# A shorter ring for gathered expert rows: seven places instead of nine

## The chip, the cores and the metric

The kernel runs on one core of one Trainium2 chip. The metric is the device time of one execution in microseconds (us), lower is better. TensorE (PE) has a matmul side and a weight-load side (PEld). VectorE is DVE, ScalarE is ACT, GpSimd is POOL, and SyncE is SP. SP issues most of the plain transfers, ACT some of them, and POOL all gathers and scatters by index. All of them run on the core's 16 DMA engines.

## The reference

One inference step of a one-layer encoder on 1024 prompt frames and 32 frames of a running stream, in float32. Per frame: one input projection; two attentions, a stick-breaking one and a latent one (MLA); a gated merge and a layer norm give `h`. Then comes the feed-forward part, in which each frame picks experts out of 16384:

```python
s = einsum('thcd,hckd->thck', q, peer_sub_keys)      # 8 heads, 2 x 128 sub-keys
s1, i1 = top_k(s[:, :, 0], 16); s2, i2 = top_k(s[:, :, 1], 16)
top_s, top_pos = top_k(s1[..., :, None] + s2[..., None, :], 16)
act = gelu(einsum('thkd,td->thk', peer_u[experts], xb))
out = einsum('thk,thkd->td', softmax(top_s) * act, peer_v[experts])
y = layer_norm(ALPHA * h + out)
```

So each frame reads 8 x 16 = 128 rows of `peer_u` and 128 of `peer_v`, of 1024 numbers each.

## The kernel before

**Two ways through the experts.** For the frames of three tiles (tiles 1, 2 and 3, 128 frames each) all 16384 experts are computed as matrix products, in 128 iterations of 128 experts. This is the last stage, `dense_experts`. In an iteration `it`, PE multiplies a block of key columns with the frames (L1809, 16 matmuls), ACT takes the gelu (L1843), DVE multiplies with gates (L1876), and 20 iterations later PE multiplies with the value rows (L1798, 12 matmuls). SP loads the key columns (512 KB), gates (192 KB) and value rows (512 KB) of every iteration. For the other five prompt tiles and the 32 frames of the stream the chosen rows are gathered: 672 gathers, each of one row of 2048 numbers (`peer_u` and `peer_v` joined, 8 KB) for each of 128 partitions, which is 1 MB.

**The ring.** A gathered row lies in a ring of `RING = 9` places. Its steps are numbered. In step s DVE first makes the dot product of row s with `h` (L574), then, `LAG = 4` steps late, adds row s-4, weighted, to the sum (L586). Between the two, ACT takes the gelu and the weight (L531, L537). L586 counts the semaphore `used`; POOL waits for it and gathers the next row into the place that came free (L431):

```python
for p, (kind, x) in enumerate(self.places):          # lay_out
    step = x + self.LAG if kind == "row" else ...
    freed.setdefault(step, []).append(p + self.RING)
...
for p in self.fetch_at.get(s, []):                   # pool
    pool.wait_ge(self.used, p - self.RING + 1)
    self.fetch(pool, p)
...
dve.wait_ge(self.got[p % self.RING], self.landed[p]) # dve_row, ahead of L574
```

**What sets the order.** The background work (the steps of the ring, and the routes) is spread over the stages of frame groups 1 and 2 and over the dense stage by the table `SHARES` and by `lay_out`. A route is the choice of 16 experts for one head of one tile: 12 small pieces of DVE work (`route_stage`, L646 to L676). It must be done when step `row` is laid out if `routed_before(row)` asks for it: `u = min(row + self.RING - self.LAG + 5, ...) // TOPK`. Where the share alone has not brought them by then, all 12 pieces stand in one block, once in 16 rows. In the dense stage part(it) hands out DVE's background work in proportion to PE's iterations. POOL runs through the same list: scores, gathers, and 384 scatters of gates (L454), in one order.

**Stick-breaking attention** (`stick_attend`) works on items of 128 x 512. PE computes scores into one of six PSUM banks (L936), ACT takes exp and ln (L1016 to L1024), DVE makes the softplus into one of `S = 6` buffers (L1048) and a running sum into one of `R = 8` (L1065), and PE adds both to the scores two pairs later (L952, L954). DVE waits with `s_done >= t - S + 1` before it writes a softplus buffer again. PE's order in turn u is: `later(2u-4)`, `later(2u-3)`, values, and then `scores(u)`, which fills items 2u and 2u+1.

Of the kernel before, what the change touches and what calls it, by code (L numbers as in the profile page):

```python
# [89 lines left out]
def hybrid_stream_step(nc, a):  # L90
# [21 lines left out]
    with ExitStack() as s:  # L112
        m["zero_done"], = sems(nc, s, "dense_gates_zeroed")
        m["x_in"], m["w0_in"], m["sig0_in"], m["sub0_in"] = sems(
            nc, s, "next_xT_in", "next_w_in_in", "next_gates_in", "next_sub_keys_in")
        m["wq_in"] = sems(nc, s, "next_wq_in_a", "next_wq_in_b")
        m["wo0_in"] = sems(nc, s, "next_w_o_in_a", "next_w_o_in_b")
        m["hTd_in"], = sems(nc, s, "dense_hT_in")
        m["out_stored"], m["mla_stored"], m["hT_stored"] = sems(nc, s, "keys_and_values_stored", "mla_stored", "dense_hT_stored")
        m["gate_stored"] = sems(nc, s, *[f"gate_stored{i}" for i in range(4)])  # L120
        m["h_stored"] = sems(nc, s, "h_stored_a", "h_stored_b")
        m["scores_stored"] = sems(nc, s, *[f"scores_stored{i}" for i in range(SCORE_STAGES)])
        m["keys_in"] = sems(nc, s, *[f"key_columns_in{i}" for i in range(5)])
        bg = Experts(nc, mem, s, a, m)
        spaces = [foreground(mem, g) for g in groups]
        for g in groups:
            f = spaces[g.n]
            project(nc, mem, a, m, f, g, bg, groups[:g.n])
            stick_attend(nc, mem, a, m, f, g, bg, groups[:g.n + 1])
            mla_project(nc, mem, a, m, f, g, bg)  # L130
            mla_attend(nc, mem, a, m, f, g, bg)
            merge_norm(nc, mem, a, m, f, g, bg)
            score_experts(nc, mem, a, m, f, g, bg, list(zip(groups, spaces))[g.n + 1:g.n + 2])
        dense_experts(nc, mem, a, m, bg)
# [34 lines left out]
class Experts:  # L169
# [1 line left out]

    RING, LAG = 9, 4
    NORM_AFTER = 10
    IDS = 176
    SLOTS, FLATS = 22, 8
# [724 lines left out]
def stick_attend(nc, mem, a, m, f, g, bg, upto):  # L902
    bg.begin(g.n, "stick")
    with ExitStack() as s:
# [6 lines left out]
                for par in range(2):  # L911
                    items.append((i, nq, key, rows, vt, diag, par, x == len(tiles) - 1))
        N = len(items)
        E, S, R, A = 4, 6, 8, 4
        work = lambda name, first, n: [mem.at(f"{name}{n * g.n + i}", FG + 38912 + 2048 * (first + i), [P, 512]) for i in range(n)]
        e = work("abs_exp_ln", 0, E)
        sp_ = work("softplus", E, S)
# [1039 lines left out]
```

## Time and profile before

| | |
|---|---|
| Median of 3 runs | 3517.1 us (3508.93 to 3527.14) |
| Span of the profiled execution | 3512.8 us, from its first to its last instruction |
| Median less that span | 4.3 us |
| PE / DVE / POOL / ACT busy | 85% / 69% / 45% / 35% |
| DMA | 1098.51 MB, mean 313 GB/s |
| Gathers (queue q0 with the scatters) | 751.05 MB |

Busy time is the union of an engine's instructions. A share of DMA of 1.00 means that all 16 engines were moving packets all the time. A releaser is the work whose end let an idle engine go on. Windows are in microseconds from the start of the span. The first matmul of the last scores stage starts at 1849, the first of the dense stage at 1959.

### The profile page before, as it was taken

How to read it: one execution, taken by the hardware profiler on the slowest of the kernel's cores; microseconds unless marked ns; L12 is line 12 of the kernel's file. 1: busy time of each engine (PE TensorE's matmuls, PEld its weight loads, DVE VectorE, ACT ScalarE, POOL GpSimd, SP SyncE). 2: the span in 40 equal slices, each digit the busy share in tenths (PEclk: the TensorE clock that was granted, in tenths of full speed). 3: DMA queues.
4: the chain of work that ended last, by engine and by line, in shares of the span. 5: the costliest groups of instructions: out<-in, count | busy, mean ns of one | idle time of the engine just before them, and what ended most of it. 6: DMA issues, size and time to landing. Idle time of an engine off the chain costs nothing. (4 is left out here: it accounts for less than half of the span.)

```text
span 3512.8 us, 36200 instructions
## 1 busy us (share of the span) xinstructions
PE 2979.5 (85%) x10191; PEld 1650.8 (47%) x10191; DVE 2437.9 (69%) x5110; ACT 1219.7 (35%) x3224; POOL 1569.2 (45%) x1186
## 2 busy tenths in 40 slices
PE   8989999775789896776799858999989999989994
PEld 5754745442445454434445534444444444444431
DVE  0122069887686878877696638878778778788878
ACT  0241234665533436765642212222222222222211
POOL 0000035667663288868766763333333333333321
PEclk9988999896899998887899979999999999999997
DMA  4675589667799997676699979999999999999996
GB/s 146 215 256 178 174 330 405 209 196 210 234 342 360 322 379 219 173 203 199 200 360 377 322 239 390 410 399 399 401 399 406 398 398 408 383 410 405 412 381 261
DMA packets 375912, 1098.51 MB, mean 313 GB/s; under 512 B 91712, under 2 KB 210208, under 8 KB 289568
## 3 DMA queue, kind: packets, MB, share of 16 engines
q0 software_dynamic: 165072, 751.05, 57.5%
q1 hardware_dynamic: 176800, 303.85, 24.6%
q10 hardware_dynamic: 33840, 41.30, 3.3%
q8 instruction: 82, 1.34, 0.1%
q14 instruction: 118, 0.97, 0.1%
HBM read 1031.97 MB, written 63.02 MB: 312 GB/s over the span
## 5 line engine op out<-in xcount | busy, mean ns | idle before, releaser
L431 POOL DMA_INDIRECT expert_rows<-in_experts,picked_index x640 | 780.9, 1220 | 1256.1 <-DVE ff_sum L586 1126.5
L586 DVE SCALAR_TENSOR_TENSOR ff_sum<-expert_rows,coefficients,ff_sum 128x1024 f32<-128x1024 f32 x672 | 860.2, 1280 | 163.1 <-ACT coefficients L537 162.0
L574 DVE SCALAR_TENSOR_TENSOR expert_rows<-expert_rows,h_tile 128x1024 f32<-128x1024 f32 x672 | 818.8, 1218 | 196.1 <-DMA expert_rows<-in_experts,picked_index 176.3
L1809 PE MATMUL dense_act_ps<-dense_hT,key_columns 128*128 128x384 f32 x2048 | 709.4, 502 | 140.7 <-DMA key_columns<-in_key_columns 116.8
L454 POOL DMA_INDIRECT gates_by_expert<-dense_gate,gate_address x384 | 681.4, 1774 | 146.6 <-issue 114.2
L1798 PE MATMUL dense_out_ps<-dense_value_rows,dense_weights 128*128 128x512 f32 x1536 | 681.1, 595 | 10.0 <-DVE dense_weights L1876 7.8
L1809 PEld LDWEIGHTS dense_act_ps<-dense_hT,key_columns 128*128 128x128 f32 x2048 | 392.7, 195 | 474.3 <-DMA key_columns<-in_key_columns 183.6
L1798 PEld LDWEIGHTS dense_out_ps<-dense_value_rows,dense_weights 128*128 128x128 f32 x1536 | 292.9, 191 | 357.6 <-issue 318.8
L842 PE MATMUL proj_ps<-xT,w_in_block 128*128 128x384 f32 (+1 forms) x1392 | 419.1, 464 | 28.8 <-PEq L1612 15.6
L842 PEld LDWEIGHTS proj_ps<-xT,w_in_block 128*128 128x128 f32 x1392 | 266.1, 192 | 180.8 <-issue 33.9
L1843 ACT ACTIVATE dense_weights<-dense_act_ps 128x384 f32<-128x384 f32 x128 | 62.5, 489 | 773.4 <-PE dense_act_ps L1809 769.4
L531 ACT ACTIVATE activated<-dots 128x1 f32<-128x1 f32 (+1 forms) x631 | 124.4, 197 | 518.8 <-DVE expert_rows L574 479.1
L1668 PE MATMUL peer_q_ps<-hT,wq_half 128*128 128x384 f32 (+1 forms) x768 | 240.9, 474 | 15.1 <-DMA wq_half<-in_peer_wq 6.9
L1668 PEld LDWEIGHTS peer_q_ps<-hT,wq_half 128*128 128x128 f32 x768 | 149.3, 197 | 97.8 <-issue 16.6
L537 ACT ACTIVATE coefficients<-activated,expert_gate 128x1 f32<-128x1 f32 x640 | 184.1, 294 | 20.2 <-ACT activated L531 0.9
L378 ACT ACT_TABLE_LOAD x110 | 141.1, 1283 | 143.0 <-DVE top_scores L663 54.3
L407 POOL DMA_DIRECT2D expert_scores<-peer_scores x72 | 67.4, 936 | 206.5 <-POOLq L1612 206.4
L1296 PE MATMUL score_ps<-mla_kT,mla_qT 96*128 96x512 f32 (+4 forms) x208 | 107.1, 638 | 39.4 <-PEq L1071 39.4
L1313 PE MATMUL mla_ps_turned<-identity,probs 128*128 128x128 f32 (+2 forms) x312 | 65.1, 326 | 83.7 <-ACT probsT L1352 78.4
L1525 PE MATMUL out_ps<-w_out,mergedT 128*128 128x512 f32 (+1 forms) x288 | 127.6, 593 | 0.0
L1048 DVE SCALAR_TENSOR_TENSOR softplus<-log_weight_ps,abs_exp_ln 128x512 f32<-128x512 f32 (+2 forms) x78 | 50.8, 651 | 104.0 <-ACT abs_exp_ln L1024 101.1
L531 ACT ACT_TABLE_LOAD x90 | 115.5, 1283 | 18.6 <-DVE expert_rows L574 15.8
(192 smaller groups left out, 2957.6 us busy)
## 6 DMA issues: line engine op xcount, KB each, us to landing
key_columns<-in_key_columns SPq DMA_DIRECT2D x128, 512.0 KB
dense_value_rows<-in_experts SPq DMA_DIRECT2D x128, 512.0 KB
gates_by_expert<-zeros POOLq DMA_DIRECT2D x12, 2048.0 KB, 21.9
wq_half<-in_peer_wq SPq DMA_DIRECT2D x48, 512.0 KB
dense_gates<-gates_by_expert SPq DMA_DIRECT2D x128, 192.0 KB
w_in_block<-in_w_in ACTq DMA_DIRECT2D x18, 1024.0 KB
w_in_block<-in_w_in SPq DMA_DIRECT2D x18, 1024.0 KB
w_out<-in_w_out SPq DMA_DIRECT2D x24, 512.0 KB, 7.2
```

Source lines behind the costliest of these rows:

```text
L378: act.preload_act_table_set(EXP_LN)
L431: pool.indirect_dma_start(to, None, self.a["experts"], bass.IndirectOffsetOnAxis(ap=index[:, k:k + 1], axis=0)).then_inc(self.got[p % self ...
L454: pool.indirect_dma_start(self.a["gates_by_expert"], bass.IndirectOffsetOnAxis(ap=self.flat[i][:, k:k + 1], axis=0), self.dgate[i][:, k:k ...
L531: act.activation(self.gel[:, k:k + m], self.dots[:, k:k + m], ACT.Gelu).then_inc(self.gelud, m)
L537: act.activation(self.coef[:, c:c + 1], self.gel[:, c:c + 1], ACT.Identity, scale=gate[:, c:c + 1]).then_inc(self.weighed, 1)
L574: dve.scalar_tensor_tensor(place, place, 1.0, self.h[n % 2][:], ALU.mult, ALU.mult, accum_out=self.dots[:, s % TOPK:s % TOPK + 1]).then_in ...
L586: dve.scalar_tensor_tensor(total, self.ring[:, p % self.RING, D:2 * D], self.coef[:, y % TOPK:y % TOPK + 1], total, ALU.mult, ALU.add).the ...
L842: mm = nc.tensor.matmul(out[:, 0:W], w[b % 2][:, k, col:col + P], xT[:, k, :], start=(k == 0), stop=(k == KC - 1))
L1525: mm = nc.tensor.matmul(ps[2 * n + c][0:r, :], f["mergedT"][:, k, at:at + r], w_out[:, k, 512 * c:512 * (c + 1)], start=(k == 0), stop=(k ...
L1668: mm = nc.tensor.matmul(qp[2 * (h % 2) + c][:, 0:W], wq[h % 4][k // 4][:, k % 4, PKEYS * c:PKEYS * (c + 1)], f["hT"][:, k, :], start=(k == ...
L1798: mm = nc.tensor.matmul(out[d][:, 512 * half:512 * (half + 1)], w[e % AB][:, P * d:P * (d + 1)], vals[e % VB][:, 512 * half:512 * (half + ...
L1809: mm = nc.tensor.matmul(up[it % 2][:, 0:W], keys[it % KB][:, k, :], hTd[:, k, :], start=(k == 0), stop=(k == KC - 1))
```

## The change

The ring of gathered rows has seven places instead of nine; `LAG` stays 4. In stick-breaking attention the softplus has four buffers instead of six, and the running sum six instead of eight. Places in memory move with them, the instructions stay the same. `routed_before` contains `RING`, so a route is demanded two rows later than before.

```diff
-    RING, LAG = 9, 4
+    RING, LAG = 7, 4
...
-        E, S, R, A = 4, 6, 8, 4
+        E, S, R, A = 4, 4, 6, 4
```

## Rows read from the trace of the kernel before

**Rows 1.** The page, busy tenths in 40 slices of the span:

```profile
PE   8989999775789896776799858999989999989994
...
DMA  4675589667799997676699979999999999999996
```

**Rows 2.** Windows: engines, granted clock, DMA share and rate by stretch:

```profile
core 0: us, PE busy (x) PEld busy (x) DVE busy (x) ACT busy (x) POOL busy (x), PEclk, DMA share, GB/s
...
1849.00:1959.00 110.00, 96.75 (x353) 61.08 (x354) 69.98 (x88) 28.53 (x98) 78.38 (x52) 0.93 1.05 383
1959.00:2165.00 206.00, 156.51 (x433) 86.31 (x434) 114.72 (x223) 44.09 (x126) 120.17 (x87) 0.88 0.86 301
2165.00:3256.00 1091.00, 1018.88 (x2689) 510.57 (x2688) 880.45 (x1599) 255.76 (x873) 388.00 (x325) 0.99 1.00 401
3256.00:3480.00 224.00, 191.85 (x464) 88.51 (x464) 184.40 (x317) 44.43 (x158) 69.08 (x60) 0.95 0.97 384
```

**Rows 3.** Groups by line in 2165:3256 (xcount, busy us, mean ns, idle before):

```profile
L1809 PE MATMUL dense_act_ps<-dense_hT,key_columns 128*128 128x384 f32 x1537 | 530.7, 499 | 78.9 <-DMA key_columns<-in_key_columns 78.8
L1798 PE MATMUL dense_out_ps<-dense_value_rows,dense_weights 128*128 128x512 f32 x1152 | 510.0, 592 | 0.0
L586 DVE SCALAR_TENSOR_TENSOR ff_sum<-expert_rows,coefficients,ff_sum 128x1024 f32<-128x1024 f32 x299 | 382.6, 1279 | 85.7 <-ACT coefficients L537 85.1 <-DVEq L620 0.5
L431 POOL DMA_INDIRECT expert_rows<-in_experts,picked_index x300 | 373.4, 1245 | 701.8 <-DVE ff_sum L586 671.7 <-issue 27.7 <-DVEq L620 2.4
L574 DVE SCALAR_TENSOR_TENSOR expert_rows<-expert_rows,h_tile 128x1024 f32<-128x1024 f32 x300 | 366.1, 1220 | 89.4 <-DMA expert_rows<-in_experts,picked_index 88.1 <-ACT activated L531 0.5
```

**Rows 4.** All instructions on expert_rows, first and last start:

```profile
L574 DVE SCALAR_TENSOR_TENSOR expert_rows<-expert_rows,h_tile x672: 1203/1217/1283, 470.3 to 3470.7; 128x1024 f32<-128x1024 f32 x168
...
L431 POOL DMA_INDIRECT expert_rows<-in_experts,picked_index x640: 937/1175/2038, 461.9 to 3460.9; - x160
```

**Rows 5.** Timeline, DVE and POOL around one route, 2675 to 2690:

```profile
2675.30 1.23 DVE L574 SCALAR_TENSOR_TENSOR expert_rows<-expert_rows,h_tile 128x1024 f32<-128x1024 f32 x1 [1.32 <-DMA expert_rows<-in_experts,picked_index]
...
2676.46 1.28 DVE L586 SCALAR_TENSOR_TENSOR ff_sum<-expert_rows,coefficients,ff_sum 128x1024 f32<-128x1024 f32 x1
...
2678.51 0.94 POOL L431 DMA_INDIRECT expert_rows<-in_experts,picked_index  x1 [2.81 <-DVE ff_sum L586]
...
2686.36 1.22 DVE L574 SCALAR_TENSOR_TENSOR expert_rows<-expert_rows,h_tile 128x1024 f32<-128x1024 f32 x1
...
2688.70 1.22 DVE L574 SCALAR_TENSOR_TENSOR expert_rows<-expert_rows,h_tile 128x1024 f32<-128x1024 f32 x1
```

**Rows 6.** Timeline of a stretch with one or two rows under way:

```profile
2030.90 1.00 POOL L431 DMA_INDIRECT expert_rows<-in_experts,picked_index  x1 [0.30 <-issue]
...
2036.50 1.22 DVE L574 SCALAR_TENSOR_TENSOR expert_rows<-expert_rows,h_tile 128x1024 f32<-128x1024 f32 x1 [3.13 <-DMA expert_rows<-in_experts,picked_index]
```

**Rows 7.** The chain that ended last, its pieces in the tail:

```profile
3437.64 12.55 DMA expert_rows<-in_experts,picked_index
...
3460.94 9.62 DMA expert_rows<-in_experts,picked_index
```

**Rows 8.** POOL's groups by line in 1849:1959:

```profile
L454 POOL DMA_INDIRECT gates_by_expert<-dense_gate,gate_address x23 | 44.3, 1925 | 7.0 <-issue 6.7 <-POOLq L1612 0.3
L431 POOL DMA_INDIRECT expert_rows<-in_experts,picked_index x29 | 36.6, 1263 | 24.9 <-DVE ff_sum L586 17.0 <-issue 7.9
```

**Rows 9.** Windows of L586 alone: stretch, length, busy (xcount), clock, DMA:

```profile
438.00:634.00 196.00, 48.63 (x38) 0.96 0.97 370
634.00:758.00 124.00, 23.08 (x18) 0.84 0.57 167
1034.00:1152.00 118.00, 34.57 (x27) 0.90 0.96 357
```

**Rows 10.** Line L1048, the softplus: what its engine waited for:

```profile
  ACT abs_exp_ln L1024: 101.1, 14
  PE log_weight_ps L954: 2.4, 1
```

## The prediction

> **What bounds the kernel now.** I read the page first, for where the time lies. From slice 24 of 40 on, DMA stands at nine tenths or more and PE at eight or nine [rows 1]; that is the dense stage, from 1959 us to the end, 44% of the span. The windows show it in numbers: from 2165 to 3256 us the DMA share is 1.00 at 401 GB/s, PE is busy 1018.88 of 1091 us, and DVE 880.45 [rows 2]. In these 1091 us PE makes 1537 / 16 = 96 iterations, so 11.36 us each; its two groups of matmuls need (530.7 + 510.0) / 96 = 10.84 us of it, and most of the rest it waits for key columns [rows 3]. DVE makes 300 steps of the ring, 3.64 us each, and is idle 88.1 us for landings and 85.1 us for coefficients [rows 3].
>
> So three things are close to each other: PE, the 16 DMA engines, and the chain of the ring. The ring's chain is the one that the change touches. POOL's gather waits 671.7 us for L586, that is for a place [rows 3]: nearly every gather in this stretch starts when a place comes free, and not when POOL has time. And the chain that ended last goes, in the tail, through just this loop: gather, landing, L574 and L586, gather [rows 7].
>
> **The loop, worked out.** A place is free at the end of L586 in step x+4, and the row that comes into it is row x+9, read in step x+9. Four whole steps lie between. With seven places it is row x+7, and two whole steps lie between: three rows per turn of the loop where five were. A turn has three terms. From the start of L574 to the end of L586 in one step: 2675.30 to 2676.46 + 1.28 = 2677.74, so 2.4 us [rows 5]. From there to the start of the gather on POOL: 2678.51 - 2677.74 = 0.8 us [rows 5]. And from the start of the gather to the L574 that reads it, which I call F. This is the unknown. Now a turn may take 5 x 3.64 = 18.2 us, which leaves 15 us for F.
>
> The trace bounds F. In a stretch where POOL hands out rows slowly, so that one or two are under way, DVE sits idle until the landing, and F is 2036.50 - 2030.90 = 5.6 us [rows 6]. The first row of all, with nothing of the ring ahead of it but with weights loading beside it, took 470.3 - 461.9 = 8.4 us; the last, with earlier rows still ahead of it and hardly any other traffic, 3470.7 - 3460.9 = 9.8 us [rows 4], and the chain's two gathers in the tail take 9.62 and 12.55 us until the landing [rows 7], the long one behind three other rows. With seven places at most two other rows can be ahead. I take 8.4 us: one row is mostly ahead, key columns are loading beside it, and the row itself keeps DMA less full than now. The ends that I keep for F are 5.6 us and 10.6 us, a third of the way from the chain's 9.62, with two rows ahead, to its 12.55.
>
> A turn is then 2.4 + 0.8 + 8.4 = 11.6 us for three rows, 3.87 us per row, while a row now has 3.64. Worse are the routes. A block of 12 pieces keeps DVE from rows once in 16 rows: the L574 before it starts at 2675.30, the one behind it at 2686.36, 11.1 us later, and the next 2.34 us after that [rows 5]. Now five rows land meanwhile and DVE works them off at 2.34 us each; with seven places three land, and the fourth comes only a turn later. Sixteen rows take 11.1 + 2 x 2.34 = 15.8 us, and 13 / 3 turns of 11.6 us = 50.3 us: 66.1 us. Now they take 16 x 3.64 = 58.2 us. That is 7.9 us more per 16 rows. The 300 rows of the stretch and, at the same pace, some 61 in the 224 us behind it are 22.6 such blocks: **+178 us**. An iteration of the dense stage becomes 66.1 / 16 x 3.125 = 12.9 us (3.125 rows per iteration now), so PE with its 10.84 us and the key columns have time; a granted clock of 0.93 as in the window from 1849 [rows 2] would be hidden as well, and no gain of PE or of key columns counts.
>
> **The stages before.** In the last scores stage 29 rows go by in 110 us, 3.79 us each, and 23 scatters of 1925 ns with 0.3 us before each stand between the gathers on POOL [rows 8], 1.8 us per row. A turn is 11.6 + 1.8 = 13.4 us, 4.5 us per row: 0.7 x 29 = +20 us. In the first 206 us of the dense stage POOL is busy 120.17 [rows 2], scatters hold up the gathers, and DVE already waits for landings; rows come two places later in POOL's line, which DVE must follow once, not in each row: +10 us. The other scores stage has 27 rows in 118 us and a projection stage 38 in 196 [rows 9], 4.4 and 5.2 us each; in these and their like (five stages) only the rows behind a route are late, some four in each by about 1 us: +20 us. A stick-breaking stage has 18 rows in 124 us [rows 9], 6.9 us each, so three rows have 20 us for a turn of 11.6; I put +10 us for all attention stages, for POOL's scatters between their gathers. Together **+60 us**, and 0 to 130 as its bounds: 0 if the foreground work in these stages hides it all, the upper if F is 10.6.
>
> **The buffers of the stick-breaking stage: 0.** PE does `later(2u-3)` before `scores(u)`, in one order. The softplus of item t = 2u or 2u+1 needs scores(u), and with S = 4 it waits for s_done >= t - 3, which is at most 2u - 2, the count that later(2u-3) has just set. So ln_done already implies it. The running sum is read last by later(t-4) with R = 6, and that is covered by the same wait. Now L1048 waited 101.1 us for ACT and 2.4 us once for PE [rows 10]; the latter is all that such a wait costs today, and I add nothing for it. No instruction is added or removed anywhere, and the routes only move by two rows; a route still ends five steps ahead of the gather that needs it, as before.
>
> The sum: 178 + 60 = +238 us. It is made against the profiled execution, whose span of 3512.8 us lies 4.3 us under the median of the runs; 3517.1 + 238 = 3755, and I say **3750 us**.
>
> **Rivals.** One: the DMA engines were the limit and stay it, and nothing changes. For it speaks the share of 1.00 [rows 2]: the bytes are the same. It needs 13 / 3 turns in 58.2 - 15.8 = 42.4 us, so a turn of 9.8 us and F at most 6.6 us. F was 5.6 us in light traffic [rows 6], so it can't be excluded, but no row under load shows it. 3517 us. The Trainium skill, DMA: Bandwidth & Descriptors, section Anatomy of one DMA — SWDGE (gpsimd) path, would have it so: about 2.0 us plus bytes over 436 GB/s, for 1 MB an estimate of 4.4 us; with 1.2 us on POOL an F of 5.6 us, a turn of 8.8 us, and no loss. By that rule the gather in light traffic agrees to the tenth [rows 6], while the last row of the trace, at 9.8 us [rows 4], doesn't: the rule is for one transfer alone.
>
> Two: partly hidden. F lies between 6.6 and 7 us and nothing is lost in the earlier stages. At F = 7.0 a turn is 10.2 us and 16 rows take 60.0 us, +41 us: 3525 to 3580 us.
>
> Three, faster: with fewer rows queued, key columns land sooner, and PE goes from 11.36 to 10.84 us per iteration, 96 x 0.52 = 50 us: 3467 us. For it speaks PE's wait of 78.8 us for key columns [rows 3]. It decides where 16 rows fit in 10.84 / 3.125 x 16 = 55.5 us: a turn of 9.2 us, F at most 6.0 us. Only light traffic shows that.
>
> Four, heavier: F stays as it is behind three rows, 12.55 us [rows 7], because key and value transfers take the share that the rows give up. A turn of 15.75 us, 16 rows in 84 us, 25.8 x 22.6 = +583 us, and 90 before it: 4190 us. Against it: fewer rows are ahead of each.
>
> **How the numbers follow.** My forecast 0.72, heavier 0.06, partly hidden 0.10, no change 0.08, faster 0.04. For the range I take F from 7.0 to 10.0 us: +41 us and +30 before it give 3588; a turn of 13.2 us, 73.0 us per 16 rows, 14.8 x 22.6 = 334 and 90 before it give 3941. The range is 3580 to 3940, which leaves out the rivals and a little of my own case beyond F = 10.0, about 2 in 10. A difference under 0.5% (18 us) can't be told from none on this kernel. Slower: 0.72 + 0.06 + 0.10 = 0.88; same 0.08; faster 0.04.
>
> **What the profile after would show.** Right: DMA share of the steady dense stretch at 0.85 to 0.93 and 350 to 375 GB/s instead of 1.00 and 401; L574's idle time for landings from 88.1 to several hundred us in the same number of rows; PE waiting for L1876 or through it instead of for key columns; behind each route two rows at 2.34 us and then a gap of about 7 us; L1048 without a wait for PE of more than a few us; the stages up to 430 us unchanged. Wrong: a DMA share that stays at 1.00, which would mean that other transfers fill what the rows leave; an F below 6.6 us; or a loss that lies in the earlier stages rather than behind the routes.

## The result and the profile after

The changed kernel takes 3779.7 us (median of 4 runs, 3763.07 to 3781.33) against 3519.3 us: a ratio of 1.0731, 95% interval 1.0705 to 1.0757. The forecast was 3750 us in a range of 3580 to 3940. The profiled execution has a span of 3779.6 us, 266.8 us more than the one before.

First the page, busy tenths in 40 slices, PE and DMA, to be held against [rows 1]:

```profile
PE   8979988766987967757897597888788888789873
...
DMA  4675599576999975666999899899889999899896
```

The run of nines on the DMA line from slice 24 on is gone; eights and nines change about. The windows say how much. Columns as in [rows 2]; the stretches are the last scores stage, the head of the dense stage, 300 rows of its steady part, and the rows after that:

```profile
1898.00:2020.00 122.00, 95.14 (x352) 60.30 (x352) 70.66 (x87) 28.63 (x98) 70.96 (x52) 0.89 1.01 357
2020.00:2222.00 202.00, 158.76 (x447) 88.00 (x448) 115.76 (x222) 43.73 (x130) 120.95 (x88) 0.90 0.87 303
2222.00:3492.00 1270.00, 1077.95 (x2708) 539.08 (x2708) 891.02 (x1602) 265.94 (x872) 366.42 (x324) 0.93 0.92 347
3492.00:3747.00 255.00, 190.48 (x431) 85.94 (x429) 183.53 (x315) 45.33 (x156) 71.39 (x62) 0.88 0.88 331
```

The steady part is 1270 us long where it was 1091, and DMA moves 347 GB/s at a share of 0.92 where it moved 401 at 1.00. PE is busy 59 us longer for 96 iterations as before, at a granted clock of 0.93 instead of 0.99. The same groups as [rows 3], in this stretch:

```profile
L1809 PE MATMUL dense_act_ps<-dense_hT,key_columns 128*128 128x384 f32 x1544 | 574.3, 530 | 154.2 <-DMA key_columns<-in_key_columns 154.2
L1798 PE MATMUL dense_out_ps<-dense_value_rows,dense_weights 128*128 128x512 f32 x1164 | 525.5, 601 | 37.9 <-DVE dense_weights L1876 37.9
L586 DVE SCALAR_TENSOR_TENSOR ff_sum<-expert_rows,coefficients,ff_sum 128x1024 f32<-128x1024 f32 x300 | 383.8, 1279 | 0.5 <-DVEq L620 0.5
L574 DVE SCALAR_TENSOR_TENSOR expert_rows<-expert_rows,h_tile 128x1024 f32<-128x1024 f32 x300 | 367.1, 1224 | 360.2 <-DMA expert_rows<-in_experts,picked_index 358.0 <-issue 0.3
L431 POOL DMA_INDIRECT expert_rows<-in_experts,picked_index x299 | 351.9, 1177 | 897.1 <-DVE ff_sum L586 854.3 <-issue 37.8 <-DVEq L620 5.1
```

L574 waits 358.0 us for landings instead of 88.1, and L586 no longer waits for coefficients (0.5 us in all instead of 85.7). The steps of the ring now wait for landings and for nothing else of note, and the gathers wait for places (854.3 us).

The measure used below is the place of the same 300 rows. This is the line of L574 from the view of all instructions on `expert_rows`, before and after; the first and last start are its two last times:

```profile
L574 DVE SCALAR_TENSOR_TENSOR expert_rows<-expert_rows,h_tile x300: 1210/1218/1283, 2164.7 to 3255.4; 128x1024 f32<-128x1024 f32 x150
```

```profile
L574 DVE SCALAR_TENSOR_TENSOR expert_rows<-expert_rows,h_tile x300: 1212/1224/1295, 2222.0 to 3489.7; 128x1024 f32<-128x1024 f32 x150
```

Before, 299 steps in 1090.7 us, 3.65 us each; after, in 1267.7 us, 4.24 us. So 177 us of the 267 lie in this stretch. Its first row comes 57.3 us later (2164.7 and 2222.0), and what remains, 33 us, lies behind it.

One route and the rows behind it, from the timeline of DVE and POOL after (start, length):

```profile
3025.98 1.23 DVE L574 SCALAR_TENSOR_TENSOR expert_rows<-expert_rows,h_tile 128x1024 f32<-128x1024 f32 x1 [0.23 <-DMA expert_rows<-in_experts,picked_index]
...
3036.67 1.23 DVE L574 SCALAR_TENSOR_TENSOR expert_rows<-expert_rows,h_tile 128x1024 f32<-128x1024 f32 x1
...
3039.02 1.22 DVE L574 SCALAR_TENSOR_TENSOR expert_rows<-expert_rows,h_tile 128x1024 f32<-128x1024 f32 x1
3039.88 1.20 POOL L431 DMA_INDIRECT expert_rows<-in_experts,picked_index  x1 [9.16 <-DVE ff_sum L586]
...
3041.83 1.22 DVE L574 SCALAR_TENSOR_TENSOR expert_rows<-expert_rows,h_tile 128x1024 f32<-128x1024 f32 x1
...
3042.22 1.65 POOL L431 DMA_INDIRECT expert_rows<-in_experts,picked_index  x1 [1.14 <-DVE ff_sum L586]
...
3045.02 0.94 POOL L431 DMA_INDIRECT expert_rows<-in_experts,picked_index  x1 [1.16 <-DVE ff_sum L586]
...
3045.53 1.22 DVE L574 SCALAR_TENSOR_TENSOR expert_rows<-expert_rows,h_tile 128x1024 f32<-128x1024 f32 x1 [1.28 <-DMA expert_rows<-in_experts,picked_index]
...
3048.43 1.23 DVE L574 SCALAR_TENSOR_TENSOR expert_rows<-expert_rows,h_tile 128x1024 f32<-128x1024 f32 x1 [0.47 <-DMA expert_rows<-in_experts,picked_index]
...
3053.70 1.23 DVE L574 SCALAR_TENSOR_TENSOR expert_rows<-expert_rows,h_tile 128x1024 f32<-128x1024 f32 x1 [2.84 <-DMA expert_rows<-in_experts,picked_index]
```

DVE is with the route from 3028 to 3036.7. Three rows have landed by then: the first is read at 3036.67, the other two 2.3 and 2.8 us later. The gather that POOL starts at 3039.88, as soon as L586 of the first is done, is read three rows on, at 3045.53: F is 5.65 us, with no other gather still to land. For the next two it is 6.2 us (3042.22 to 3048.43) and 8.7 us (3045.02 to 3053.70), each time with DVE idle until the landing. This route is one of the quick ones; the section on why the prediction was right has the means. The chain that ended last goes through the same loop in the tail, with landings of 5.86 to 9.44 us where [rows 7] had 9.62 and 12.55:

```profile
3663.09 9.44 DMA expert_rows<-in_experts,picked_index
...
3698.64 7.29 DMA expert_rows<-in_experts,picked_index
...
3718.39 5.96 DMA expert_rows<-in_experts,picked_index
...
3731.62 5.86 DMA expert_rows<-in_experts,picked_index
```

### The profile page after: what moved, and what is told of

Its sections match the earlier page's. It is cut to its first block and busy times, and to the rows that moved or that the text cites. A ratio compares the mean times of both kernels' runs of the same rounds, so it can differ in the third digit from the quotient of the medians.

```text
span 3779.6 us, 36207 instructions
## 1 busy us (share of the span) xinstructions
PE 3047.4 (81%) x10191; PEld 1681.4 (44%) x10191; DVE 2454.7 (65%) x5110; ACT 1230.2 (33%) x3224; POOL 1518.9 (40%) x1186
## 5 line engine op out<-in xcount | busy, mean ns | idle before, releaser
L431 POOL DMA_INDIRECT expert_rows<-in_experts,picked_index x640 | 735.7, 1150 | 1570.2 <-DVE ff_sum L586 1402.8
L574 DVE SCALAR_TENSOR_TENSOR expert_rows<-expert_rows,h_tile 128x1024 f32<-128x1024 f32 x672 | 821.1, 1222 | 673.8 <-DMA expert_rows<-in_experts,picked_index 630.2
L1809 PE MATMUL dense_act_ps<-dense_hT,key_columns 128*128 128x384 f32 x2048 | 751.1, 525 | 232.4 <-DMA key_columns<-in_key_columns 185.7
L586 DVE SCALAR_TENSOR_TENSOR ff_sum<-expert_rows,coefficients,ff_sum 128x1024 f32<-128x1024 f32 x672 | 860.0, 1280 | 23.8 <-ACT coefficients L537 22.5
L1798 PE MATMUL dense_out_ps<-dense_value_rows,dense_weights 128*128 128x512 f32 x1536 | 699.6, 607 | 73.9 <-DVE dense_weights L1876 73.9
L1809 PEld LDWEIGHTS dense_act_ps<-dense_hT,key_columns 128*128 128x128 f32 x2048 | 416.4, 206 | 580.0 <-DMA key_columns<-in_key_columns 231.2
L842 PE MATMUL proj_ps<-xT,w_in_block 128*128 128x384 f32 (+1 forms) x1392 | 427.1, 470 | 41.9 <-PEq L1612 22.2
L1048 DVE SCALAR_TENSOR_TENSOR softplus<-log_weight_ps,abs_exp_ln 128x512 f32<-128x512 f32 (+2 forms) x78 | 50.8, 651 | 101.2 <-ACT abs_exp_ln L1024 96.4
```

Source lines behind the costliest of these rows:

```text
L431: pool.indirect_dma_start(to, None, self.a["experts"], bass.IndirectOffsetOnAxis(ap=index[:, k:k + 1], axis=0)).then_inc(self.got[p % self ...
L574: dve.scalar_tensor_tensor(place, place, 1.0, self.h[n % 2][:], ALU.mult, ALU.mult, accum_out=self.dots[:, s % TOPK:s % TOPK + 1]).then_in ...
L586: dve.scalar_tensor_tensor(total, self.ring[:, p % self.RING, D:2 * D], self.coef[:, y % TOPK:y % TOPK + 1], total, ALU.mult, ALU.add).the ...
L842: mm = nc.tensor.matmul(out[:, 0:W], w[b % 2][:, k, col:col + P], xT[:, k, :], start=(k == 0), stop=(k == KC - 1))
L1798: mm = nc.tensor.matmul(out[d][:, 512 * half:512 * (half + 1)], w[e % AB][:, P * d:P * (d + 1)], vals[e % VB][:, 512 * half:512 * (half + ...
L1809: mm = nc.tensor.matmul(up[it % 2][:, 0:W], keys[it % KB][:, k, :], hTd[:, k, :], start=(k == 0), stop=(k == KC - 1))
```

## The experiments

Of each edit only what differs from the kernel before is shown. The ratios are to the kernel before on the same chip.

**The ring alone, and the buffers alone**

```diff
-    RING, LAG = 9, 4
+    RING, LAG = 7, 4
```

> Ring of seven, buffers of the stick-breaking stage as before (six and eight). Loop theory (a turn of the ring bounds the rows, the buffers cost nothing): the whole loss, ratio 1.070 to 1.076, some 3775 us. Rival, the buffers share in the loss: under 1.068.

```diff
-        E, S, R, A = 4, 6, 8, 4
+        E, S, R, A = 4, 4, 6, 4
```

> Ring of nine as before, softplus buffers four and later sums six. Loop theory: no change, ratio 0.998 to 1.002, and L1048 waits for PE not more than a few us. Rival, the softplus now waits for PE: above 1.003, with the loss between 150 and 185, 640 and 760, and 1350 and 1530 us.

The ring alone: 3773.7 us, 1.0736 (1.0710 to 1.0762), the whole loss. The buffers alone: 3517.8 us, 1.000 (0.9988 to 1.0012). With both parts, this is all that L1048 waited for beside 4.5 us of issue, where [rows 10] had 2.4 us for PE:

```profile
  ACT abs_exp_ln L1024: 96.4, 14
```

So the second half of the change costs nothing that these runs can see.

**Places or gathers per turn**

A ring of nine in which the sum follows six steps behind has again three rows to a turn, but all nine places.

```diff
-    RING, LAG = 9, 4
+    RING, LAG = 9, 6
```

> Nine places, but the weighted sum follows six steps behind the dot product instead of four, so that again only three gathers belong to a turn of the loop, with all nine places in use. Loop theory: as slow as the ring of seven, 1.065 to 1.085. Rival, it is the number of places or their addresses in memory that counts: 1.00.

3800.1 us, 1.080 (1.0774 to 1.0826). The line of L574 (301 rows) and what it waited for:

```profile
L574 DVE SCALAR_TENSOR_TENSOR expert_rows<-expert_rows,h_tile x301: 1212/1225/1268, 2236.6 to 3523.9; 128x1024 f32<-128x1024 f32 x151
...
  DMA expert_rows<-in_experts,picked_index: 367.6, 188
```

4.29 us per row, and nearly the waits of the ring of seven. All nine places at their old addresses don't help; what counts is how many gathers belong to a turn: RING - LAG. This run is still 0.6% slower than the ring of seven (1.080 and 1.0736, the intervals don't meet), and no run shows why.

**The moved routes**

```diff
-        u = min(row + self.RING - self.LAG + 5, self.n_rows - 1) // TOPK
+        u = min(row + 10, self.n_rows - 1) // TOPK
```

This goes with the ring of seven.

> Ring of seven, but a route is demanded as many rows ahead as with nine places (row + 10), so that the order of rows and routes is that of before. Loop theory: as the ring of seven, 1.070 to 1.076. Rival, the loss comes from the moved routes: back to 1.00 to 1.02.

3794.1 us, 1.0784 (1.0756 to 1.0811), a little over its expected band. To move the routes back doesn't help; it costs 20 us more than the ring alone, and no run shows why.

**Eight places and six**

```diff
-    RING, LAG = 9, 4
+    RING, LAG = 8, 4
```

> Eight places: four rows per turn. Loop theory: with 9 to 10.5 us from the gather's start to the step that reads it a turn is 12.2 to 13.7 us, 16 rows take 10.9 + 3 x 2.34 + 12 / 4 turns = 54.5 to 59 us against 58.7 with nine places, so most of the loss is gone: ratio 1.00 to 1.02. Rival, the loss grows evenly with each place: 1.036.

```diff
-    RING, LAG = 9, 4
+    RING, LAG = 6, 4
```

> Six places: two rows per turn. Loop theory: with less ahead of it a gather takes 7 to 7.5 us to the step that reads it, a turn 10.2 to 10.7 us, 5.1 to 5.35 us per row; 16 rows take 10.9 + 2.4 + 14 / 2 turns = 84.5 to 88 us against 58.7 with nine places, 580 to 660 us over 361 rows, and 150 to 250 us in the stages before: ratio 1.21 to 1.26. Rival, each place taken away costs about what the last did (6.5%): 1.14.

Eight: 3543.0 us, 1.0084 (1.0062 to 1.0105), as the loop theory had it. Six: 4443.0 us, 1.2643 (1.2602 to 1.2684), at the upper end of its band or just over it. L574 with eight places, then with six:

```profile
L574 DVE SCALAR_TENSOR_TENSOR expert_rows<-expert_rows,h_tile x300: 1210/1225/1294, 2160.9 to 3278.0; 128x1024 f32<-128x1024 f32 x150
...
  DMA expert_rows<-in_experts,picked_index: 196.9, 183
```

```profile
L574 DVE SCALAR_TENSOR_TENSOR expert_rows<-expert_rows,h_tile x300: 1215/1225/1278, 2414.5 to 4075.1; 128x1024 f32<-128x1024 f32 x150
...
  DMA expert_rows<-in_experts,picked_index: 743.2, 249
```

In this table a turn is the mean time per row times the rows of a turn, so a share of the routes is in it. The row of seven places is the changed kernel. F is its mean over the rows between routes, that is without the first RING - LAG rows behind each route, which had landed during it; it is taken from the starts of all gathers and of all L574 in the timelines, the n-th gather with the n-th L574. It has in it what a landed row still waits for DVE, above all with nine places, where DVE waits for a landing in only 90 of the 300 rows:

| places | rows per turn | us per row | turn, us | F, us | ratio |
|---|---|---|---|---|---|
| 9 | 5 | 3.65 | 18.2 | 12.1 | 1 |
| 8 | 4 | 3.74 | 14.9 | 9.9 | 1.008 |
| 7 | 3 | 4.24 | 12.7 | 8.2 | 1.073 |
| 6 | 2 | 5.55 | 11.1 | 6.9 | 1.264 |

With fewer rows queued each is read sooner after its gather has started, and the turn gives way: by 3.3 us from nine places to eight, by 2.2 to seven, by 1.6 to six. From nine to eight that makes up for nearly all of the row that a turn has lost, further on for less and less of it. The even loss per place is refuted at both ends (0.8% and 19 points instead of 3.6% and 6.5).

**Routes piece by piece**

In the dense stage the pieces of a route are spread over 16 rows: what `lay_out` demands grows row by row.

```diff
+                if block[0] == len(GROUPS) and row < end:
+                    due = self.routed_evenly(row + m - 1, due)
...
+    def routed_evenly(self, row, due):
+        ahead = row + self.RING - self.LAG + 5
+        u, part = ahead // TOPK, ahead % TOPK
+        if u + 1 >= len(self.units):
+            return due
+        more = (self.route_of_unit[u + 1] - self.route_of_unit[u]) * self.N_STAGES
+        return due + max(0, more) * (part + 1) // TOPK
```

> Ring of seven, ring only; in the dense stage the 12 pieces of a route no longer stand in one block but one by one between the steps of 16 rows. Loop theory: without the blocks 16 rows take 16 / 3 turns of 11.6 to 12 us, 62 to 64 us instead of 68, so some 100 us of the loss come back: ratio 1.035 to 1.05. Rival, the turns alone make the loss and the blocks cost nothing beyond their own DVE time: 1.07 as before.

> The same spreading of the routes with nine places. Loop theory: five landed rows already cover a block of route pieces, so nothing is gained beyond 0.5%: 0.995 to 1.003. Rival, the blocks cost DVE or PE time in any case: 0.98 or less.

Seven places: 3713.5 us, 1.0559 (1.0538 to 1.0580). That is 60 us less than the ring of seven with its blocks, in the right direction but not the 100 us expected, and outside both bands. Nine places: 3510.2 us, 0.998 (0.9954 to 1.0006), no difference, as expected. L574 with seven places and spread routes (301 rows):

```profile
L585 DVE SCALAR_TENSOR_TENSOR expert_rows<-expert_rows,h_tile x301: 1199/1225/1296, 2205.5 to 3434.0; 128x1024 f32<-128x1024 f32 x151
...
  DMA expert_rows<-in_experts,picked_index: 347.6, 184
```

16 rows take 65.5 us (4.095 x 16) instead of 67.8. So in the steady part it costs some 2.3 us per 16 rows that the pieces stand in one block. The other 65.5 - 58.4 = 7.1 us are not the turns by themselves: DVE still has to do the 12 pieces, and they now lie between the rows. F is 8.8 us here over all rows, where it is 8.2 us between the blocks of the changed kernel.

**Half the bytes**

Each gather brings 4 KB per partition of a table seen as 32768 rows, and the weighted sum reads the half that holds the product; the output is therefore not the reference's. Done with nine places and with seven.

```diff
-        pool.indirect_dma_start(to, None, self.a["experts"], ...
+        pool.indirect_dma_start(to[:, 0:D], None, self.a["experts"].rearrange("e (x c) -> (e x) c", x=2), ...
...
-            dve.scalar_tensor_tensor(total, self.ring[:, p % self.RING, D:2 * D], ...
+            dve.scalar_tensor_tensor(total, self.ring[:, p % self.RING, 0:D], ...
```

> Nine places; each gather brings 4 KB per partition instead of 8 (one row of 1024 numbers of a table seen as 32768 rows), and the weighted sum reads the same half, so the output is not the reference's. The gathers' bytes are halved. If DMA throughput holds the dense stage with nine places, PE becomes the limit at 10.84 us per iteration: 50 to 90 us less, ratio 0.97 to 0.985. If it doesn't, 0.99 to 1.00.

> The same halved gathers with seven places. Loop theory: from the gather's start to the step that reads it now 6 to 6.5 us, a turn of 9.2 to 9.7 us, 16 rows in 56 to 58 us, near PE's 55.5: ratio to before 0.98 to 1.00, and 1.01 to 1.02 to nine places with halved gathers. Rival, the two places are missed for another reason than the landing: 1.05 or more over nine places with halved gathers.

Nine places: 3347.3 us, 0.9518 (0.9499 to 0.9537). Seven: 3537.6 us, 1.0052 (1.0035 to 1.0069), and 1.057 of the other (3537.6 / 3347.3). Both are outside what was expected. The steady window of nine places with half the bytes, columns as in [rows 2]:

```profile
2124.00:3119.00 995.00, 989.96 (x2682) 508.08 (x2681) 874.42 (x1602) 256.47 (x875) 390.30 (x325) 1.00 0.81 284
```

PE is busy 989.96 of 995 us: this is PE's floor, 995 / 96 = 10.4 us per iteration at a granted clock of 1.00, less than the 10.84 us on which expectation and prediction built. Those 10.84 us add up two groups of matmuls that overlap: the union of PE's busy time in [rows 2], 1018.88 us, is 10.6 us per iteration. So the transfers did hold the kernel before, and by more than they were taken for. That it was what the DMA engines can move, and not the time of a turn, is borne out by the run with a delay and nine places further down: 1.8 us more in each turn cost its steady part only 11 us. L574 in both, nine places first:

```profile
L574 DVE SCALAR_TENSOR_TENSOR expert_rows<-expert_rows,h_tile x300: 1205/1218/1251, 2123.9 to 3116.8; 128x1024 f32<-128x1024 f32 x150
...
  DMA expert_rows<-in_experts,picked_index: 10.4, 15
```

```profile
L574 DVE SCALAR_TENSOR_TENSOR expert_rows<-expert_rows,h_tile x300: 1214/1224/1276, 2150.9 to 3276.1; 128x1024 f32<-128x1024 f32 x150
...
  DMA expert_rows<-in_experts,picked_index: 224.4, 114
```

With seven places L574 waits 224.4 us for landings, with nine 10.4 us: the two places are missed for the landing, also with half the bytes. The comparison of the totals, at 1.057, meets the number that was set for the rival, since the case with nine places went down to PE's floor; it doesn't tell the theories apart, the waits do. What was wrong is how much F gives way: 3.76 us per row are a turn of 11.3 us, only 1.4 us less than with all bytes, and F between routes went from 8.2 to 6.6 us. If the other half of the bytes is worth as much, an estimate, they are 3.3 of the 8.2 us, and most of F is not the moving of the row's own bytes.

**A delay that moves no byte**

After each wait for a place POOL sets 128 cells four times in a row before it starts the gather.

```diff
                     pool.wait_ge(self.used, p - self.RING + 1)
+                    for _ in range(4):
+                        pool.memset(self.idle[:], 0.0).then_inc(self.idled, 1)
+                        self.n_idled += 1
+                        pool.wait_ge(self.idled, self.n_idled)
```

> Seven places, and before each gather that waits for a place POOL sets 128 cells four times in a row, which holds the gather back by 1.0 to 1.2 us and moves no byte. Loop theory: the delay goes into each turn, a third of it into each row: 0.33 to 0.4 us x 361 rows of the dense stage, some 120 to 145 us, and 20 to 50 us in the stages before, ratio 1.11 to 1.13. Rival, DMA throughput sets the rows with seven places too: 1.073 to 1.085.

> The same delay with nine places. Loop theory: a turn has 18.2 us and needs less, so the delay is hidden in the dense stage; POOL's own line grows by 1.1 us per gather where it is busy with scatters: ratio 1.00 to 1.015. Rival, any later gather is paid for: 1.03 or more.

Seven places: 4128.8 us, 1.1737 (1.1712 to 1.1761). Nine: 3778.7 us, 1.0754 (1.0733 to 1.0774). Both far above what was expected, and for nine places above the rival's threshold. The timeline of POOL with nine places shows what the edit really costs:

```profile
2703.13 0.99 POOL L399 MEMSET idle_cells<- 128x128 f32 x4 [7.09 <-DVE ff_sum L592]
2704.89 1.36 POOL L437 DMA_INDIRECT expert_rows<-in_experts,picked_index  x1 [0.78 <-POOL idle_cells L399]
```

That is 0.99 us of work and 0.78 us of waits between, 1.8 us per gather instead of 1.0 to 1.2. L574 with nine places and with seven, each with the delay:

```profile
L580 DVE SCALAR_TENSOR_TENSOR expert_rows<-expert_rows,h_tile x300: 1212/1224/1285, 2411.6 to 3513.5; 128x1024 f32<-128x1024 f32 x150
```

```profile
L580 DVE SCALAR_TENSOR_TENSOR expert_rows<-expert_rows,h_tile x300: 1212/1225/1295, 2478.6 to 3822.9; 128x1024 f32<-128x1024 f32 x150
```

In the steady part nine places hide it: 1101.9 us instead of 1090.7, 3.69 us per row. Seven don't: 1344.3 instead of 1267.7 us, +0.26 us per row, so 0.77 us per turn. That is what the theory says of the dense stage, though less than half of the 1.8 us went into the mean turn. The starts in the two timelines show where the rest is: between routes the gather starts 1.6 us later in the turn than without the delay (5.1 us after the start of the L574 before it instead of 3.5), and F is 0.7 us shorter (7.5 instead of 8.2). Why a delayed row lands sooner was not tried; the DMA share fell from 0.92 to 0.88. The stages before are what made the totals: with nine places the steady part begins at 2411.6 us instead of 2164.7, with seven at 2478.6 instead of 2222.0, 247 and 257 us later. 316 gathers start there, 1.8 us each would be some 560 us, and POOL in the kernel before had only this much waiting for places to give in all of 438 to 2165 us (in the steady part it is 671.7 us for 300 gathers):

```profile
POOL expert_rows L431 <- DVE ff_sum L586: 373.5, 95, 23.9
```

So the delay can't be hidden there, and both expectations put it far too low (at most 1.5% of the time with nine places, 20 to 50 us with seven).

## Why the prediction was right, and where it was off

**The loop.** That a place frees in step x+4, that two whole steps and not four then lie ahead of its next reader, and that this bounds the rows, is what the runs show: the ring alone has the whole loss, and nine places with six steps of lag have it as well. 16 rows were put at 66.1 us; measured were 4.24 x 16 = 67.8 us. The dense stage's steady part lost 177 us where 7.9 x 300 / 16 = 148 were forecast, the rest of it 33 us where 30 were.

**Its two parts.** The stretch has 18 whole periods of 16 rows, from one route to the next, 68.1 us each on the mean of the starts in the timelines. The block of the route and the two rows behind it take 10.8 + 2.5 + 3.0 = 16.3 us where 15.8 were put. The other 13 rows take 3.98 us each where 3.87 were put: a turn of 11.9 us instead of 11.6. In it the gather starts 3.5 us after the start of L574 (3.2 were put, which is the median), and F is 8.2 us on the mean, where 8.4 were taken. So terms and sizes both came out. That F was met to 0.2 us is partly luck: it was read off the very first gather of the kernel, and in the stretch it goes from 5.5 to 11.6 us. Directly behind a route, where mostly none of the ring's gathers is still to land, it is shorter, 5.65 to 8.92 us and 6.9 on the mean, and the gap there is 4.9 us on the mean (3.7 in the timeline shown) where about 7 was forecast; the same 8.4 us had been put there.

**What the prediction had not asked** is what a route costs when it does not stand in a block. Its 66.1 us are 16 x 3.87 = 61.9 us for the turns and 4.2 for the block, which would mean that without a block the pieces vanish into the waits for landings. With the routes spread, 16 rows took 65.5 us: only 2.3 us come back.

**The stages before.** +60 us were forecast for everything up to the steady part, 57.3 us came. The distribution was different: the last scores stage became 12 us longer (110 to 122) where 20 were put, the head of the dense stage 4 us shorter (206 to 202) where 10 were put, and the stages ahead of them 49 us longer instead of 30 (the last scores stage starts at 1898 and not at 1849). That the sum is met is luck: errors of 8, 14 and 19 us cancel.

**The buffers** at nothing: confirmed, 1.000. Ahead of the ring nothing moved either: the first row is read at 469.1 us where it was 470.3.

**DMA.** A share of 0.85 to 0.93 and 350 to 375 GB/s were forecast; it is 0.92 and 347, just under the band. The rival that DMA throughput stays the limit needed F at 6.6 us or less, and loses: 16 rows in 67.8 us, with DMA not full. With nine places, though, it was the limit: half the bytes took 98 us off the steady part. The Trainium skill's rule for one transfer (DMA: Bandwidth & Descriptors, Anatomy of one DMA — SWDGE (gpsimd) path) gave an F of 5.6 us; the trace has 5.65 us just behind the route shown and 8.7 us two gathers later, and on the mean 6.9 us behind a route and 8.2 us between routes. The rule gives about the shortest F, and not that of a turn.

**A step that failed: PE and the key columns.** It was forecast that PE would wait for L1876 instead of for key columns. L1876 did appear, with 37.9 us, but the wait for key columns doubled, from 78.8 to 154.2 us, although DMA had room. SP's own waits in the steady part, first after, then before:

```profile
SPq L1765 <- DVE dense_weights L1876: 732.3, 82, 24.4
SPq L1770 <- PE dense_out_ps L1798: 399.0, 55, 15.7
```

```profile
SPq L1770 <- PE dense_out_ps L1798: 818.1, 92, 17.0
SPq L1765 <- DVE dense_weights L1876: 145.9, 37, 12.6
```

SP stands at L1765, the gates of a block, until DVE's L1876 frees a buffer: 732.3 us where it was 145.9. The value rows and the next key columns are issued behind it in the same line. When DVE is late with rows, so are the key columns. With six places, where DVE is later still, PE's wait has gone over to L1876 as forecast: 402.1 us for it and 101.0 for key columns. The faster rival needed an F of 6.0 us at most and fails by that alone; but fewer rows in the queue don't bring key columns sooner either if their issue waits for DVE. Whether this costs anything beyond what the rows cost already is not shown: the link is read from the waits and from the order in the code, and no run took it apart.

**What stays open.** What F is made of. Half the bytes took 1.6 of its 8.2 us off; the rest was not split. Open are also the 20 us that the old place of the routes costs, the 0.6% between nine places with a lag of six and seven places, and what the late key columns cost.

## What to carry to other kernels

The depth of a ring is not its number of places but the places less those that are held back for a later use; a turn has that many loads. Compare what a turn needs (use, release, issue, landing) with the time that so many rows have at the present pace, and remember that a load is read later when more are queued (12.1 us after its start with five to a turn, 8.2 with three): from 9 to 8 places that gave nearly all of it back, from 8 to 7 it no longer could. Where the consumer has blocks of other work, look at the rows behind them, but expect shorter landings there (6.9 us here) than within a turn, and don't expect the work's own time to vanish when it is spread.

## What the runs showed of the hardware that was not expected

A gather of 8 KB for each of 128 partitions was read 5.65 to 8.92 us after its start, directly behind a route, with mostly nothing of the ring still to land; between routes it was 6.9, 8.2, 9.9 and 12.1 us on the mean with two, three, four and five gathers to a turn, with what a landed row waits for DVE in it. Halving its bytes shortened a turn of 12.7 us by only 1.4. With half the bytes and nine places PE was busy 989.96 of 995 us at a granted clock of 1.00. When PE waited more for its data, the granted clock of the steady part went from 0.99 (PE busy 93% of 1091 us) to 0.93 (85% of 1270 us), and the mean matmul of L1809 from 499 to 530 ns; whether that cost any time no run shows. And 1.8 us more of POOL per gather, hidden in the dense stage (+11 us), moved the start of the steady part by 247 us in the stages in which POOL also scatters.
